# ScalarE's key scaling put behind the turned keys of a segment, its decays ahead of the last squares, and partial-result stores awaited half by half

## The reference

```python
q = silu(qb) * 128 ** -0.5
f = lb + (1 - lb) * sigmoid(fb)          # forget gate
k = 1 - f
S_t = diag(f_t) S_{t-1} + k_t i_t^T      # o_t = S_t^T q_t
o_n = o_b * rsqrt(mean(o_b ** 2) + EPS) * norm_g
```

## Time and profile before

| | |
|---|---|
| median of three runs | 1555.66 us |
| profiled execution | 1562.63 us |
| its span | 1560.8 us |
| mean granted TensorE clock | 0.984 of full |
| TensorE busy | 1506.6 us, 97% |
| VectorE, ScalarE, GpSimd busy | 49%, 32%, 28% |
| DMA traffic | 338.34 MB, mean 217 GB/s |
| recurrence of the prompt, from the first group behind the projection | about 885 to 1038 us |
| attention | about 1039 to 1342 us |

### The profile page before, as it was taken

How to read it: one execution, slowest core, us unless ns; L and a number is a source line. 1 busy time by engine, 2 the same in 40 slices (tenths; PEclk the granted TensorE clock), 3 DMA queues, 4 the chain that set the end, 5 groups by cost and what they waited for, 6 DMA issues and landing times.

```text
span 1560.8 us, 25524 instructions
## 1 busy us (share of the span) xinstructions
PE 1506.6 (97%) x9802; PEld 1348.0 (86%) x9802; DVE 768.2 (49%) x1941; ACT 502.0 (32%) x1426; POOL 440.1 (28%) x281
## 2 busy tenths in 40 slices
PE   7999999998999999989999999989899999999996
PEld 7999999997588777767778899989899999888885
DVE  6121120002423222222226699857677777898884
ACT  5111111112210113312222132357577777432231
POOL 0333210000150000100000100038797688344442
PEclk9999999999899999999999999999999999999998
DMA  9999998142694957967471399679698962966741
GB/s 302 332 325 345 340 330 243 41 143 91 187 326 146 325 194 248 334 230 253 154 253 48 79 290 339 199 231 200 153 195 194 195 166 77 315 209 206 221 158 54
DMA packets 174501, 338.34 MB, mean 217 GB/s; under 512 B 15635, under 2 KB 115283, under 8 KB 165523
## 3 DMA queue, kind: packets, MB, share of 16 engines
q1 hardware_dynamic: 141452, 169.18, 35.9%
q10 hardware_dynamic: 22432, 111.29, 22.1%
q0 software_dynamic: 10512, 56.48, 13.4%
HBM read 262.25 MB, written 155.39 MB: 268 GB/s over the span
## 4 chain that ended last, share of the span: by engine, by line
PE 63%; DVE 4%; DMA 4%; ACT 2%; issue 1%; POOL 1%; SPq 0%; DVEq 0%; ACTq 0%; POOLq 0%
PE banks L759 22%; PE banks L1878 11%; PE banks L1843 7%; PE banks L1815 5%; PE banks L1154 4%; PE banks L1829 4%; DMA spare<-in_xT 2%; PE banks L826 1%; DMA partials<-a_stage 1%; DVE at L1102 1%; PE banks L808 1%; PE banks L1859 1%; PE banks L1144 1%; DVE kf L1081 1%; PE banks L1199 1%
## 5 line engine op out<-in xcount | busy, mean ns | idle before, releaser
L256 PE MATMUL acc<-xhi,whi 128*128 128x424 f32 (+1 forms) x640 | 227.9, 356 | 8.7 <-DVE xlo L235 8.7
L759 PE MATMUL banks<-nwhi,nxhi 128*128 128x512 f32 (+1 forms) x544 | 220.6, 405 | 13.3 <-DVE nwlo L494 6.9
L256 PE MATMUL acc<-xlo,whi 128*128 128x424 f32 (+1 forms) x640 | 227.4, 355 | 0.0
L256 PE MATMUL acc<-xhi,wlo 128*128 128x424 f32 (+1 forms) x640 | 227.4, 355 | 0.0
L1453 POOL CAST a_sorted<-a_plain 128x2048 fp32r<-128x2048 f32 x45 | 171.1, 3856 | 167.0 <-DVE at L1102 132.9
L759 PE MATMUL banks<-nwhi,nxlo 128*128 128x512 f32 (+1 forms) x544 | 214.5, 394 | 0.0
L759 PE MATMUL banks<-nwlo,nxhi 128*128 128x512 f32 (+1 forms) x544 | 214.2, 394 | 0.0
L1718 ACT ACTIVATE a_prob<-a_prob,a_stage 128x256 f32<-128x256 f32 (+1 forms) x384 | 174.1, 454 | 80.0 <-DVE a_stage L1561 78.0
L1561 DVE CUSTOM_DVE_ANT_0 a_prob<-banks,a_bias 128x256 f32<-128x256 f32 (+1 forms) x384 | 125.2, 364 | 80.7 <-PE banks L1815 73.0
L1843 PE MATMUL banks<-a_v,a_probT 128*128 128x64 f32 x1200 | 157.7, 269 | 4.9 <-DVE a_probT L1573 4.9
L1843 PEld LDWEIGHTS banks<-a_v,a_probT 128*128 128x128 f32 x1200 | 150.0, 193 | 6.6 <-DVE a_probT L1573 6.0
(11 more groups left out here) (212 smaller groups left out, 2537.1 us busy)
## 6 DMA issues: line engine op xcount, KB each, us to landing
a_plain<-split_qk POOLq DMA_DIRECT2D x48, 512.0 KB, 13.2
out_kwin_s<-in_cache_kT ACTq DMA_DIRECT2D x8, 2048.0 KB, 20.0
split_qk<-spare POOLq DMA_DIRECT2D x16, 1024.0 KB, 14.4
spare<-in_xT SPq DMA_DIRECT2D x32, 512.0 KB, 7.0
projN<-nstage SPq DMA_DIRECT2D x32, 512.0 KB, 5.5
qg<-in_cache_kT ACTq DMA_DIRECT2D x8, 2048.0 KB, 11.6
kf<-in_cache_v ACTq DMA_DIRECT2D x8, 2048.0 KB
out_kwin_s<-in_cache_kT ACTq DMA_DIRECT2D x8, 2032.0 KB, 29.7
```

The lines of the kernel that those rows point to most:

```text
L256: mm = pe.matmul(acc[:, j, 0:n], w[:, u, k], x[:, k, c0:c0 + n], start=(k == 0 and a == 0), stop=(k == KD - 1 and a == 2))
L759: mm = pe.matmul(acc[0:m, n % 2], x[:, u, k, 0:m], w[:, k, g * H:(g + 1) * H], start=(k == 0 and b == 0), stop=(k == KD - 1 and b == 2))
```

## The change

In the recurrence, `decays` is dissolved. `keys(s + 2)` moves from behind all outputs of segment s to right behind the four copies of its turned keys, ahead of the first read-out copy; the wait for `t_done`, which the copies have already passed, goes. `forgets(s + 2)` moves ahead of the last chunk's squares, with the wait for the state's last update of the segment. In the attention, the first of the two transfers of c = 0 and c = 2 gets a semaphore of its own, `half_free`; VectorE waits for that one at b = 0 and for the second at b = 8. SP waits for both kinds ahead of `load_partials(1)`.

```diff
@@ hgrn_prompt, scalar @@
-            def decays(s):
-                u = s % 2
-                act.wait_ge(s_done, NCK * (s - 1) + 1)
-                act.wait_ge(t_done, NCK * (s - 1))
-                keys(act, s, range(HB))
-                forgets(act, s, range(HB))
-
             def squares(s, c):
...
                 if s >= 2:
                     act.wait_ge(ost_free[u], 16 * (s // 2))
+                if s + 2 < NSEG:
+                    keys(act, s + 2, range(HB))
                 for c in range(NCK):
                     act.wait_ge(o_done, NCK * s + c + 1)
                     nc.scalar.activation(ost[u][:, c], o_ps[:, c % 2], ACT.Copy).then_inc(o_out, 1)
+                    if c == NCK - 1 and s + 2 < NSEG:
+                        act.wait_ge(s_done, NCK * (s + 1) + 1)
+                        forgets(act, s + 2, range(HB))
                     if s < NSEG - 1:
                         squares(s, c)
 
             for s in range(NSEG):
                 outputs(s)
-                if s + 2 < NSEG:
-                    decays(s + 2)
                 for n in range(FIRST_COPIES + 2 * s, min(FIRST_COPIES + 2 * s + 2, 2 * NB)):
                     shift_window(act, win, n, copied)
@@ attend_and_project @@
-    PIECES = (2, 4, 2)
+    PIECES = (1, 4, 1)
...
+        half_free = [sem(f"a_half_free{m}") for m in range(2)]
...
                     for half in range(2):
                         m = NBK // 2
                         sp.dma_start(a[:, half * m:(half + 1) * m], b[:, half * m:(half + 1) * m]
-                                     ).then_inc(stage_free[c], 16)
+                                     ).then_inc(stage_free[c] if half else half_free[c // 2], 16)
...
             for c in range(NC):
                 sp.wait_ge(stage_free[c], 16 * PIECES[c] * (NG if c else NG - 1))
+            for m in range(2):
+                sp.wait_ge(half_free[m], 16 * (NG if m else NG - 1))
             load_partials(1)
...
-                if x == 0 and b == 0 and g >= 1:
+                if x == 0 and b == 0 and g >= 1 and c != 1:
+                    dve.wait_ge(half_free[c // 2], 16 * g)
+                if x == 0 and b == (0 if c == 1 else NBK // 2) and g >= 1:
                     dve.wait_ge(stage_free[c], 16 * PIECES[c] * g)
```

## The result

The changed kernel takes 1572.88 us (median of six runs, 1570.41 to 1574.33) beside 1553.61 us of the kernel before (six runs, 1552.06 to 1557.06): a ratio of 1.0119, with a 95% interval of 1.0103 to 1.0134. On 1553.61 us that is 18.5 us slower, between 16.0 and 20.8. The forecast was +16.1 us. The profiled execution took 1572.51 us, its span 1570.7 us at a mean clock of 0.982, so it is close to the median.

What follows compares the result with a forecast made beforehand. TensorE, busy 97% of the span, was taken to bound the kernel, with a recurrence chain without slack. 18.25 + 2.5 − 2.42 − 2.2 = +16.1 us gave 1571.8 us; forecast 1566 to 1577 (chance 0.62), range 1561 to 1580.

Steps and rivals of the forecast that it cites:

- The mechanism: Recurrence: ScalarE's `keys` waits for the segment's load, holding back read-out copies; TensorE's third read-out comes late, not caught up.
- Segment 0's outputs: Recurrence, first stop: load lands at 917.39, read-out 8.48 us late; taken in by the second stop, not added.
- Segment 1's outputs: Recurrence, second stop: load lands at 971.97, read-out 18.25 us late, TensorE standing about 8 to 10 us.
- Clock: TensorE behind the second stop: work at the lower clock, 1.2 of 2.4 GHz, loses 2.5 us.
- Start of segment 3: Recurrence: keys and decays ready early let segment 3 start like segment 2, −2.42 us; bounds −2.4 and 0.
- Stores: Attention: VectorE waits only for the first of two partial-result transfers, −2.2 us; bounds 0 and −3.9.
- Decays ahead of the squares: Recurrence, ScalarE: decays put 2.91 us ahead of squares nobody waits for; zero, or 2.9 us without that cover.
- The sum: Whole kernel: +16.1 us, from 18.25 + 2.5 − 2.42 − 2.2.
- the issue at 961 isn't made later: Recurrence: SP, still held by its own earlier issues, issues segment 3's load no later; landing kept at 972.
- the other half of the argument: Recurrence: work ahead of segment 3's load on the shared DMA engines is the same in sum, so landing stays 972.
- The second rival: Recurrence: segment 3's load lands 10 us earlier, at 962, window copies out of SP's way; +6.4 us, 1562.1; chance 0.19.
- The first rival: Recurrence: loads land before ScalarE's next duty, leaving only the gains; −4.6 us, 1551.0; chance 0.07.

Runs made afterwards that it cites:

- experiment 2: The kernel before with `keys` alone moved behind the turned keys, decays, squares and stores as before: 1575.26 us against 1555.81, ratio 1.0116.
- experiment 12: The changed kernel's recurrence part whole, but with stores awaited as in the kernel before: 1576.92 us against 1554.71, ratio 1.0129.
- Experiment 4: The changed kernel with the loads of segments 2 and 3 both issued earlier: 1552.22 us against 1555.81, ratio 0.9981.
- experiment 9: The changed kernel with window copies spread as none, two, two and one piece behind segments 0 to 3: 1581.78 us against 1554.8, ratio 1.0175.
- Experiment 8: The changed kernel with segment 0's four window copies issued behind segment 1's outputs instead: 1579.19 us against 1554.65, ratio 1.015.
- experiment 5: The changed kernel with only segment 2's load issued earlier: 1564.36 us against 1554.65, ratio 1.0054.
- experiment 3: The kernel before with only the stores awaited per half: 1552.38 us against 1555.81, ratio 0.9982.
- experiment 7: The changed kernel with `keys` late, beside the decays ahead of the last squares: 1549.63 us against 1554.65, ratio 0.9966.
- experiment 10: The changed kernel with `keys` beside the decays ahead of the last squares and both loads issued early: 1550.25 us against 1554.8, ratio 0.9977.

## Why the prediction was right

**The mechanism** was the forecast's at each step: `keys` holds the wait for the load, the wait heads off ScalarE's copies, the third read-out needs the first copy, and what is lost isn't caught up.

**Segment 0's outputs.** Forecast 8.48 us late. The load landed at 913.1, 4.3 us earlier by the clock of the span than assumed. Against the start of the recurrence, which is 2.17 us earlier in this profile, the read-out at 916.73 is 916.73 − 912.59 + 2.17 = 6.3 us late, 2.2 less than forecast, since the load landed 29.5 us behind that start and not 31.6. The stop is 6.16 us, not 8. This term is not in the sum, so the error stayed out of it.

**Segment 1's outputs.** Forecast 18.25 us late. Measured 973.15 − 957.40 + 2.17 = 17.9 us. The stop of 9.96 us lies in the forecast 8 to 10. That the 8.48 us are not added to the 18.25 is confirmed in this way: the lateness is set by the landing, and the first stop is a part of it. The 17.9 us are made up of 6.2 and 10.0 us of standing and some 1.6 us of low clock behind the first stop (the stretches from 917 to 921). It holds only as long as the transfers don't run dry during the first stop; in the profiles of experiments 2 and 12 they did, and the landing moved by some 3 us. The forecast had no term for that, and left out the first stop's low clock as taken in by the second wait.

**Clock.** Forecast 2.5 us, measured 2.4 us behind a stop of 9.96 us. The other profiles show how wide this term is: 2.2 us behind 10.07 us (experiment 2) and 4.4 behind 8.9 us (experiment 12). The forecast's reading of the rows is off a little: in the earlier trace rows the lower level lasts to 979.2 (978 to 980 has 0.70), not to 978.6.

**Start of segment 3.** Forecast −2.42 us. VectorE's timeline of the changed kernel:

```profile
992.95 0.73 DVE L1098 COPY_PREDICATED at<-lmask,banks 128x512 f32<-128x512 int32 x1
993.59 2.33 DVE L1069 TENSOR_TENSOR qd<-qg,kf 128x1024 f32<-128x1024 f32 x2
...
999.99 0.69 DVE L1076 TENSOR_TENSOR qd<-qd,kf 128x512 f32<-128x512 f32 x1 [0.91 <-PE banks L1150]
```

From the last `keep` to the first `widen` it is 999.99 − 992.95 = 7.04 us, exactly segment 2's figure in the earlier trace rows, where the earlier trace rows had 9.46; the kernel before had 8.76 when profiled again, so the gain is 1.7 to 2.4 us. Experiment 4 shows the term by itself, −2.0 us of recurrence.

The three together: 17.9 + 2.4 − 2.4 = 17.9, and the recurrence is 17.8 us longer than in the first profile, 18.2 than in the mean of the three. The forecast's 18.25 + 2.5 − 2.42 = 18.33 is right.

**Stores.** Forecast −2.2 us, VectorE's wait from 5.2 to 3.0. Measured 3.1 and, by themselves, −2.8 us (−4.8 to −0.9). The profiles show more: from the last turn to the end of the span it is 536.7 to 538.9 us in the five kernels with the old stores and 529.1 to 534.8 in eight with the new ones (the ninth is experiment 9, whose attention is disturbed), some 6 us apart in the mean. Most of that can be placed. VectorE's wait for partial results is 4.2 to 5.5 us with the old stores and 0 to 3.1 with the new ones, 3.2 us less in the mean, and the time lost to the lower clock in that stretch (length times the share of the clock that was missing) is 10.5 us against 7.0 in the mean. The low clock behind the wait for partial results itself cost 3.4 us in the first profile of the kernel before, 1.7 in the changed kernel, and nothing in five of the eight, whose waits were 2.0 us or less. The forecast had put that gain in its bound (−3.9) and not in its sum, so the term is, if anything, too small. The ratio decides on the time; why it shows 2.8 us where the profiles show 6 stays open.

**Decays ahead of the squares.** Forecast zero, measured 1.0001 (0.999 to 1.0011).

**The sum**, +16.1 us, lies at the lower end of the measured 16.0 to 20.8. The terms of the recurrence are right to half a microsecond against this one profile. Against the two other profiles of the same edit they are 3 to 5 us short (+21.6 and +22.9 us), by the longer low clock and the later landing. So the close agreement is in part luck: the profiled execution was one in which the lower clock was short and the transfers did not run dry. The 2.4 us between the forecast and the measured median may be a share of such executions; no run here shows that.

**One step's reason was wrong, though its number held.** The prediction said of segment 3's load that "the issue at 961 isn't made later". It was made 32 us earlier, at 929.28, and at 932.45 and 930.70 in experiments 2 and 12. SP was not held by its own earlier issues: it had got through its attention loads by 922 and issued at once when `store(0)` was free. In the kernel before, SP was held from 916 to 958 by the issues themselves: 25.0 us for four loads of values, 10.3 for the next one and 6.3 for `store(0)`, with the window copies in the queues from 922.23 on. Here the copies came 5 us later, and SP was through. The landing stayed because of the other half of the argument, that the work ahead of the load on the shared engines is the same in sum: the load now stood among the window copies issued in the microseconds around it, which are two pieces, four transfers of 2 MB each, so 8 MB. From the first turned keys to the landing the transfers moved 24.9 MB before (289 GB/s over 86.2 us) and 24.2 MB after (282 GB/s over 85.9 us). Experiment 8 shows it: the same early issue, copies away, landing after 12.7 us. The Trainium skill's page "DMA: Bandwidth & Descriptors", section "Issuing engines are not separate DMA queues", says that transfers issued by different engines run on the same engines and interleave, and these runs agree: 12.7 against 40.2 us. The second rival (landing at 962) had half of that rule: the copies out of the way would do it, but they were not out of the way.

**The first rival**, the loads landing before ScalarE's duty, would have given −4.6 us. Its condition, made true by hand in experiment 4, gave −3.0 us. The fit that spoke for it, 2 us and the bytes over 436 GB/s, is from the same page of the Trainium skill, section "Anatomy of one DMA — SWDGE (gpsimd) path", which gives it for transfers that GpSimd issues. For some transfers it comes close: the page of the kernel before has a median of 4.9 us for twelve stores of 1056 KB to `projT`, issued by SP, where an estimate from the fit is 4.5. For the loads of segments 2 and 3 it doesn't hold: 1 MB took from 9.1 (experiment 5, the second of segment 2's) to 40.2 us, by what else was in the queues.

## What to carry to other kernels

An instruction that is moved up into a hole takes its waits with it, and on an engine with one stream the wait holds everything behind it. Look up when the awaited transfer lands, not how long the hole is; if the landing lies behind the hole, bring the load forward first, or leave the instruction where it was. Two stops that end at landings are not independent: what repairing one gives back depends on when the other load then lands. Here it was 10.1 of 18.5 us, because the repair also took 2 MB out of the other load's way. To foretell a landing among busy queues, count the bytes ahead of it, and ask whether the transfers run dry before the next ones are issued. Of the whole change the part worth keeping is the store awaited by halves (−2.8 us); with it, the kernels of experiments 3, 7 and 10 (0.9982, 0.9966, 0.9977) all beat both kernels, and their intervals overlap.

## What the runs showed that I had not expected

- **When a transfer is issued says little about when it lands in a loaded stretch.** Issued at 929.28 it took 40.2 us, issued at 961.17 it took 10.8 us, and both landed within 2.5 us of each other. The bytes moved until then decide: 24.9 and 24.2 MB, and 22.1 MB where the landing came 7.5 us sooner.
- **An issue isn't free to the engine that makes it.** Single issues of ScalarE took 0.52 to 2.02 us (experiment 7) where two pieces of window copies (four issues) stood together, and 6.97 and 9.21 us in a row of eight, with ScalarE's computing held for 21.11 us. SP's four loads of values took 6.51 us or 34.54 us to issue, by what was in the queues. The Trainium skill's page "DMA: Bandwidth & Descriptors", section "Issuing engines are not separate DMA queues", calls the time to initiate a transfer "usually small relative to the DMA itself". It was small for the first four issues of experiment 8 (0.58 to 1.32 us) and not for the fifth, sixth and eighth, so an engine on the critical path shouldn't issue many large transfers in a row.
- **Bulk copies that nobody waits for still have a place.** Moved behind segment 1 they held ScalarE (+23.3 us), spread over segments 1 to 3 they held the attention's loads (+27.2 us); both kernels came out slower than the changed one, though its stop of 10 us was gone.
- **What a stop costs in low clock varies more than its length.** Stops of 6.2, 6.9 and 7.2 us at the same read-out were followed by 3.1, 9.0 and 9.1 us at the lower level (the changed kernel, experiments 2 and 12). The lower clock before the window copies was what let the transfers run dry in the latter two.
